# Projections finished by token block, K, Q and V in another order, and a router that reads raw x

## The reference

```python
h = modulate(rms_norm(x, norm_mix[0]), sh_m, sc_m)      # h * (1 + scale) + shift
x = x + g_m * retention(h, ...)                          # ends in (silu(g) * on) @ ret_w_out
x = x + g_f * swiglu(modulate(rms_norm(x, norm_ff[0]), sh_f, sc_f), ff_w_in, ff_w_out)
k, v = split(modulate(rms_norm(x, kv_norm), sh_kv, sc_kv) @ kv_w)
h = modulate(rms_norm(x, norm_mix[1]), sh_m1, sc_m1)
x = x + g_m1 * stick_breaking(h, k, v, sb_w_q, sb_w_out) # 16 heads of 64, strictly causal
h = modulate(rms_norm(x, norm_ff[1]), sh_f1, sc_f1)
logits = h @ router                                      # top 2 of 8 experts, softmax of the two
x = x + g_f1 * sum_e gate[:, e] * swiglu(h, moe_w_in[e], moe_w_out[e])
return rms_norm(x, final_norm)
```

## Time and profile before

| | |
|---|---|
| median of 3 runs | 1656.91 us (1653.4 to 1657.97) |
| the profiled execution | 1656.74 us, span 1655.0 us |
| TensorE busy | 1562.3 us, 94% |
| VectorE busy | 1407.4 us, 85% |
| ScalarE busy | 1074.0 us, 65% |
| GpSimd busy | 59.6 us, 4% |
| mean granted clock of TensorE | 0.976 |
| moved by DMA | 500.91 MB, mean 303 GB/s |

### The profile page before, as it was taken

How to read it: one execution, slowest core, us unless ns; L and a number is a source line. 1 busy time by engine, 2 the same in 40 slices (tenths; PEclk the granted TensorE clock), 3 DMA queues, 4 the chain that set the end, 5 groups by cost and what they waited for, 6 DMA issues and landing times.

```text
span 1655.0 us, 22753 instructions
## 1 busy us (share of the span) xinstructions
PE 1562.3 (94%) x7324; PEld 1296.9 (78%) x7324; DVE 1407.4 (85%) x1537; ACT 1074.0 (65%) x1164; POOL 59.6 (4%) x47
## 2 busy tenths in 40 slices
PE   5999997999979896999999999999999999999996
PEld 4788775888869665888888888888888888888884
DVE  6988987788887745898998998998998998999994
ACT  3454433444355535787787787787887877878783
POOL 0212200000000110000000000000000000000000
PEclk9999998999989996999999999999999999999998
DMA  9977776788847321899999999999999999999991
GB/s 333 348 249 263 253 272 219 254 309 297 317 164 268 102 77 51 325 388 347 358 376 345 359 368 355 358 372 356 349 376 348 358 379 343 362 373 338 366 380 53
DMA packets 235114, 500.91 MB, mean 303 GB/s; under 512 B 9744, under 2 KB 40640, under 8 KB 235072
## 3 DMA queue, kind: packets, MB, share of 16 engines
q1 hardware_dynamic: 233904, 500.29, 83.9%
q10 hardware_dynamic: 1168, 0.07, 0.0%
HBM read 499.28 MB, written 1.05 MB: 302 GB/s over the span
## 4 chain that ended last, share of the span: by engine, by line
PE 83%; DVE 8%; issue 3%; DMA 2%; ACT 2%; POOL 1%; DVEq 0%; SPq 0%; ACTq 0%; POOLq 0%
PE ps L492 24%; PE ps L494 24%; PE ps L493 24%; DVE w_lo L1358 2%; DVE acc L1377 2%; DMA ada<-in_ada_w 2%; PE ps L908 1%; PE ps L726 1%; PE ps L730 1%; PE ps L728 1%; DMA raw<-in_ret_w_in 1%; PE ps L525 1%; PE ps L917 1%; PE ps L941 0%; PE ps L918 0%
## 5 line engine op out<-in xcount | busy, mean ns | idle before, releaser
L1358 DVE TENSOR_TENSOR w_lo<-raw,w_hi 128x1024 fp32r<-128x1024 f32 x834 | 994.2, 1230 | 83.5 <-ACT w_hi L1006 69.4
L1006 ACT ACTIVATE w_hi<-raw 128x1024 fp32r<-128x1024 f32 x834 | 865.6, 1060 | 254.7 <-PE ps L494 216.8
L492 PE MATMUL ps<-w_hi,RA 128*128 128x512 f32 x1528 | 607.2, 397 | 12.0 <-DVE w_lo L1358 2.9
L494 PE MATMUL ps<-w_hi,RA 128*128 128x512 f32 x1528 | 598.5, 392 | 0.0
L493 PE MATMUL ps<-w_lo,RA 128*128 128x512 f32 x1528 | 597.9, 391 | 0.0
L492 PEld LDWEIGHTS ps<-w_hi,RA 128*128 128x128 f32 x1528 | 288.7, 189 | 71.5 <-issue 3.2
L494 PEld LDWEIGHTS ps<-w_hi,RA 128*128 128x128 f32 x1528 | 288.5, 189 | 61.6
L493 PEld LDWEIGHTS ps<-w_lo,RA 128*128 128x128 f32 x1528 | 288.9, 189 | 58.4 <-issue 0.5
L492 PE MATMUL ps<-w_hi,hT_hi 128*128 128x512 f32 x400 | 160.6, 401 | 7.7 <-DVE hT_lo L1428 6.9
L494 PE MATMUL ps<-w_hi,hT_lo 128*128 128x512 f32 x400 | 157.4, 393 | 0.0
L493 PE MATMUL ps<-w_lo,hT_hi 128*128 128x512 f32 x400 | 157.3, 393 | 0.0
(11 more groups left out here) (232 smaller groups left out, 1021.7 us busy)
## 6 DMA issues: line engine op xcount, KB each, us to landing
raw<-in_moe_w_in SPq DMA_DIRECT2D x224, 1024.0 KB
raw<-in_moe_w_out SPq DMA_DIRECT2D x112, 1024.0 KB
ada<-in_ada_w SPq DMA_DIRECT2D x46, 1024.0 KB, 7.3
raw<-in_ff_w_in SPq DMA_DIRECT2D x44, 512.0 KB
raw<-in_ret_w_in SPq DMA_DIRECT2D x16, 1024.0 KB
raw<-in_ff_w_out SPq DMA_DIRECT2D x11, 1024.0 KB
raw<-in_ret_w_in SPq DMA_DIRECT2D x16, 512.0 KB
raw<-in_ret_w_out SPq DMA_DIRECT2D x8, 1024.0 KB
```

The costliest lines, as they stand in the source:

```text
L492: pe.matmul(out, a_hi, b_hi, start=first, stop=False)
L494: return pe.matmul(out, a_lo, b_hi, start=False, stop=last)
L1006: act.activation(w_hi[:, cn % RING, cols], raw[:, cn % RAW, cols], ACT.Copy).then_inc(hi_done, 1)
L1358: v.tensor_tensor(w_lo[:, cn % RING, cols], raw[:, cn % RAW, cols], w_hi[:, cn % RING, cols].bitcast(f32), ALU.subtract).then_inc(lo_done, 1)
```

## The change

Projections by block: the last halves of each output projection are gone through for block 0, then for block 1, and gating, root, norm, transposes and modulation are done per block. The transposes of a block are put between matmuls of the other. The first tile after it goes by block too.

```diff
-            for m in range(8):
+            for m in range(5):
...
+            block_rows(U_OUT + 5, rT_hi, rT_lo, 10, 0, 0, False, False)
+            pe.wait_ge(gbc_ev, 1)
+            reduce_ada(11, 4)
+            pe.wait_ge(rTl_ok, PAIRS)
+            block_rows(U_OUT + 6, rT_hi, rT_lo, 12, 0, 0, False, False)
+            block_rows(U_OUT + 7, rT_hi, rT_lo, 14, 0, 0, False, True).then_inc(y_ok, 1)
+            block_rows(U_OUT + 5, rT_hi, rT_lo, 10, 1, 2, False, False)
+            reduce_ada(12, 5)
+            block_rows(U_OUT + 6, rT_hi, rT_lo, 12, 1, 2, False, False)
+            transpose_x(1, 0)
+            block_rows(U_OUT + 7, rT_hi, rT_lo, 14, 1, 2, False, True)
...
+                    block_half(c, 0, 0, 0, 1)
+                    transpose_x(1, 1)
+                    block_half(c, 1, 0, 0, 1)
+                    block_half(c, 0, 1, 1, 1)
+                    block_half(c, 1, 1, 1, 1)
```

VectorE's order there (ScalarE's follows it), with all eight steps of unit 13 behind block 1:

```diff
-            woven(26, 0, (8, 12), 12, (0, 6))
+            woven(26, 0, (8, 12), 12, (0, 8))
             mod_out(11, 4)
...
+            add_gated(0, 0, gate_m, f_tmp)
+            split_quarters(U_FF, 0, 0, 1)
+            normed(1, 0)
+            split_quarters(U_FF, 0, 1, 2)
             mod_out(12, 5)
...
+            modulate(1, 1, 0, FF0 + SH)
+            split_quarters(U_FF, 0, 2, 3)
+            add_gated(0, 1, gate_m, f_tmp)
+            split_quarters(U_FF, 0, 3, 4)
+            normed(1, 1)
+            split_quarters(U_FF, 0, 4, 6)
+            modulate(1, 1, 1, FF0 + SH)
+            ada_steps(13, 0, 8)
```

```diff
+            halves = [(kv_w, h, D) for h in range(2)]
+            halves += [(w, h, t * TW) for t in range(2) for w in (kv_w, sb_w_q[0]) for h in range(2)]
+            halves += [(kv_w, h, D + TW) for h in range(2)]
+            halves += [(sb_w_out[0], h, t * TW) for h in range(2) for t in range(2)]
+            ada_after = {0: (22, 0), 1: (22, 1), 3: (23, 0), 4: (23, 1), 6: (24, 0), 8: (24, 1), 10: (25, 0), 11: (25, 1),
+                         13: (26, 0), 14: (26, 1)}
...
+            out_block(0, 0)
+            out_block(0, 1).then_inc(y_ok, 1)
+            pe.wait_ge(gbc_ev, 3)
+            reduce_last(25)
+            reduce_last(26)
+            out_block(1, 0)
...
+            transpose_raw(0)
+            out_block(1, 1)
...
+            route(0)
+            transpose_raw(1)
             broadcast_gate(3, diag3, 2)
+            route(1)
```

The buffers of the pairs rotate over three places instead of four, the gate's diagonal moves on GpSimd from before the masks to between masks 5 and 6. The router multiplies raw x (transposed by `transpose_raw`) by router weights that carry scale and gain (`rws`), multiplies by the reciprocal root and adds the shift's part (`sh_e`) afterwards:

```diff
+                    last = pe.matmul(ps[:, 6 + b, 0:NE], h32[:, b, kc, :], rws[:, kc, :], start=kc == 0,
+                                     stop=kc == KC - 1)
...
+                ins = v.scalar_tensor_tensor(logit[:, b, :], ps[:, 6 + b, 0:NE], stat[:, 6 + b:7 + b], sh_e, ALU.mult,
+                                             ALU.add)
```

```diff
             def gathered_high(ne):
                 act.wait_ge(hgT_done, ne + 1)
-                act.activation(hg_hi.rearrange("p (n c) s -> p n (c s)", n=2), ps[:, 6:8, :], ACT.Copy)\
-                   .then_inc(hgh_ok, 1)
+                for c in range(4):
+                    ins = act.activation(hg32[:, c, :], ps[:, 6, c * P:(c + 1) * P], ACT.Identity,
+                                         bias=modc[:, FF1 + SH + c:FF1 + SH + c + 1], scale=scol[:, 4, c:c + 1])
+                ins.then_inc(hg32a_ok, 1)
+                act.wait_ge(hg32a_ok, ne + 1)
+                act.activation(hg_hi[:, 0:4, :], hg32[:, 0:4, :], ACT.Copy).then_inc(hgh_ok, 1)
+                act.wait_ge(hg32b_ok, ne + 1)
+                act.activation(hg_hi[:, 4:8, :], hg32[:, 4:8, :], ACT.Copy).then_inc(hgh_ok, 1)
...
             def gathered_low(ne):
-                dve.wait_ge(hgh_ok, ne + 1)
-                v.tensor_tensor(hg_lo.rearrange("p (n c) s -> p n (c s)", n=2), ps[:, 6:8, :],
-                                hg_hi.rearrange("p (n c) s -> p n (c s)", n=2).bitcast(f32),
-                                ALU.subtract).then_inc(hgl_ok, 1)
+                dve.wait_ge(hgT_done, ne + 1)
+                for c in range(4, KC):
+                    ins = v.tensor_scalar(hg32[:, c, :], ps[:, 7, (c - 4) * P:(c - 3) * P], scol[:, 4, c:c + 1],
+                                          modc[:, FF1 + SH + c:FF1 + SH + c + 1], ALU.mult, ALU.add)
+                ins.then_inc(hg32b_ok, 1)
+                for i in range(2):
+                    dve.wait_ge(hgh_ok, 2 * ne + i + 1)
+                    v.tensor_tensor(hg_lo[:, 4 * i:4 * i + 4, :], hg32[:, 4 * i:4 * i + 4, :],
+                                    hg_hi[:, 4 * i:4 * i + 4, :].bitcast(f32), ALU.subtract).then_inc(hgl_ok, 1)
```

More of the change, by code:

```diff
@@ L41 @@
 U_KV = U_FF + 3 * FT
[L42 to L44 removed]
+U_SBO = U_KV + 12
 U_MOE = U_SBO + 4
@@ L603, in pair_of_heads @@
                     pe.wait_ge(mod_ok, 2 * i + 1)
-                tile(0, m, (0, 1), None if later else 0)
+                if later:
+                    tile(0, m, (0, 1))
+                else:
+                    tile_by_blocks(0, (0, 1), 0)
                 if later:
@@ new lines, in route @@
+            def route(b):
+                pe.wait_ge(xra_ok, b + 1)
+                pe.wait_ge(xrb_ok, b + 1)
+                for kc in range(KC):
+                    last = pe.matmul(ps[:, 6 + b, 0:NE], h32[:, b, kc, :], rws[:, kc, :], start=kc == 0,
+                                     stop=kc == KC - 1)
+                last.then_inc(rt_done, 1)
+            transpose_raw(0)
+            out_block(1, 1)
+            pe.wait_ge(rws_ok, 1)
+            pe.wait_ge(xra_ok, 1)
+            pe.matmul(ps[:, 6, 2 * NE:3 * NE], ones[:, :], shw[:, :], start=True, stop=True)
@@ L1343, in _ @@
                 y_high(ne)
-            root_mean_square(4)
+            root_table()
+            for b in range(NB):
+                root_mean_square(4, b)
         @block.vector
@@ L1724, in _ @@
+            steps.link(ins)
             for b in range(NB):
```

681 lines of the change are left out of this document (367 added, 314 removed).

## The result

The changed kernel takes 1626.38 us (median of 4 runs, 1625.24 to 1628.77), the kernel before 1656.28 beside it (1653.4 to 1657.97): ratio 0.9825, 95% interval 0.9809 to 0.9841. Forecast were 1637 us and a range of 1628 to 1650. The profiled execution took 1626.12 us, span 1624.4.

The account below looks back on a forecast made before the run. TensorE was taken as the bound, with serial chains behind projections as its waits and VectorE having little room. 0.6 - 2.6 - 6.5 - 10.5 + 0 - 0.6 = -19.6 from 1656.9 gave 1637 us, range 1628 to 1650.

Parts of the forecast that it names:

- Part 1: First tile by blocks: four scalings of 128 columns on ScalarE, not two of 256, before the first matmul: +0.6 us.
- Part 2: Retention projection into the dense mixer: -4.2 us by VectorE's queue, less 1.6 charged for clock: -2.6 us.
- The clock's 1.6: Charge of 1.6 us for low clock behind the two waits of some 4 us before the first SwiGLU product.
- Parts 3 and 4: Dense mixer into K, Q, V, then attention: shorter waits let the output projection end sooner, together -6.5 us.
- Part 5: Router and gather: 24 us instead of 34.5 from the last projection matmul to the first expert matmul: -10.5 us.
- Part 6: Experts: added scalings and lows on VectorE (+1.8 us per expert) and ScalarE (+2.0) fit the room: 0 us.
- Part 7: End of the kernel: the first block's root and scaling lie beside the second's square: -0.6 us.
- (b): Better covered than counted: attention's waits vanish (-6 us) and the broadcast runs at full clock: 1628 us, chance 0.11.
- (a): Short waits keep the clock down and VectorE's queue sets the pace: +8 us, 1645 us, chance 0.19.
- (c): Block 1's chain starts as late as both blocks' did, and routing waits anyway: within 5 us of 1657, chance 0.05.
- (d): Scaling in the experts overruns its room, so TensorE waits in each of 7 experts: +27 us, 1664 us, chance 0.07.

Follow-up runs that it names:

- before_again: The kernel before, unchanged, profiled a second time: median 1654.38 us, span 1651.3 us.
- after_scale_twice: The changed kernel with the eight scalings of each gathered block made twice, the first time into a spare place: 1631.83 us.
- after_warm: The changed kernel with idle transposes of the unit matrix put into six of TensorE's waits, some 70% of each: 1620.55 us.
- before_warm: The kernel before with idle transposes of the unit matrix in seven of TensorE's waits: 1645.21 us.
- after_rows_whole: The changed kernel with the last three halves of the retention's output projection gone through for both blocks together again: 1634.04 us.
- after_out_first: The changed kernel with all matmuls of attention's output projection before block 0's transposes: 1632.68 us.
- after_tile_first: The changed kernel with TensorE taking the very first tile through both blocks together, once both are scaled: 1632.06 us.
- before_diag_late: The kernel before with GpSimd making the first gate's diagonal only after the last silu of the gates: 1650.35 us.

## Why the prediction was wrong

The waits went where each part said, and the sum was 10.6 us short. Two steps of it failed: the execution that it starts from, worth 3.6 us, and the prices of its terms, worth 7.0. Had the sum started from before_again (1653.0 us), the same terms would have given 1633.4 and a range down to 1624.4, with 1626.4 inside; from that kernel's median of 1654.4 they would have given 1634.8 and 1625.8. By its own steps, with the misses of the table:

- **Part 1 and what stands before it, 3.4 us: the step that failed most.** "+0.6" held at its place (43.92 to 44.61). But I made the sum against one execution, which lay 0.2 us from a median of three runs, as if it were typical. Two w_lo of 2.32 and 2.92 us in it were an accident, as before_again shows: there the w_lo of 240.89 comes at 236.89, so that the first line of the table reads +1.2 (0.6 above its forecast) and not -2.8, and every later stage is as long as in the table within 0.2 us. Of the 4.0 us, 2.4 are there at the wait of 205.15, and 1.6 are the slow starts behind it, which also come without a long w_lo (after_scale_twice). I used them as a price of the clock and never looked at what VectorE did before. Against before_again's span (1651.3) the change gains 26.9 us.
- **Part 2, 2.2 us, the largest of the mis-sized terms.** VectorE's chain from the first quarter to the first SwiGLU transposes took 40.4 us, not 42.6. The scalings of 128 columns had no row, and I took 0.44 and 0.40 where 0.37 and 0.34 were paid; with their lows and waits they took VectorE 2.7 us for each block, where the sum has 3.4 and 2.9 (1.0 us). The first four quarters with eight product steps took 10.1 us, not 10.7: quarters last 1.23 us but the next instruction starts after 1.14, and the sum adds whole durations there, and 1.2 us for each of the eight quarters behind. The clock's 1.6 came as 1.5. The two waits measured 3.80 and 2.97 where I said some 4 each.
- **Parts 3 and 4, 1.5 us.** V starts 14.6 us behind the mixer's last half, as forecast within 0.4. The waits in attention sum to 6.2 us, where 6.7 were counted and 8 charged with handovers: the charge on top was wrong, and the half us that I took off for it was too little.
- **Part 5, 1.3 us.** 22.7 us, forecast 24 of 23.3 to 25.2. Gate and add (2.8), the transposes (1.8) and the routing (1.9) came as forecast, and the broadcast held TensorE for 2.45 us (607.84 to 610.29) against 1.9 to 3.8. The wait of the top-2 chain was 2.15 and not 2.7, and from the counting to the first expert matmul 11.7 us passed, not 12.2.
- **Part 6, 1.0.** TensorE's 123 us per expert held. The gain is clock at the first expert's start: 9 slow starts for 14.
- **Part 7, 1.4.** The last matmuls behind the wait of 2.89 us ran 1.1 us sooner by the clock (seven slow starts for thirteen), which the sum didn't have and nothing here explains. What is left for the roots' order is 0.9, not 0.6; no run tests it alone.

The misses of parts 2 to 5 share a sign, because at each open price I took the dearer end and then added handovers; those of parts 1, 6 and 7 share it by the accident and the clock. That 1637 was too high by 10.6 rather than 7 is therefore bad luck. Of the rivals, (b) named the right side with the wrong places: attention's waits didn't vanish, and the broadcast did not run wholly at the full clock. (a) fell: after_warm shows that 5.3 us of clock could be had back in the changed kernel, but the kernel before pays more of it (8.5 us in before_warm). (c) and (d) fell with the result itself; after_rows_whole and after_out_first show that the overlap by blocks is real, and after_scale_twice that the experts had room.

## To carry to other kernels

Cut the chain behind a projection by token block and put one block's chain beside the other's matmuls: here two such places cost 8 and 7 us when the overlap was taken back. At the very first tile the same cut cost 0.7 us. Before making a sum against one execution, take a second execution, look for instructions of a common shape that took twice their group's mean, and ask what GpSimd did there. Where a wait can't be removed, fill most of it with harmless matmuls: 5 us here for six lines, 8.5 in the kernel before.

## What was not expected of the hardware

- Two executions of the same program differed by 4.0 us at 237 us of the span: 2.4 by the order in which VectorE and GpSimd started (GpSimd's product 0.03 us ahead of one VectorE instruction or 0.18 behind another), 1.6 by slow starts behind it.
- A wait of 2.18 or 2.19 us before the same matmuls cost clock in some executions and none in others: slow starts behind it in 3 of 10 traces (before, after_scale_twice, after_tile_first), none in the other 7, the changed kernel, after_warm and after_rows_whole among them. So too behind the 1.22 us at the dense mixer's first tile (ten slow starts in before_again, none in before_diag_late). It is worth 1.6 to 2.1 us a time, as much as several of the edits here gain. What decides it stays open; no run here tells.
- Small matmuls at a wait's side can be worth their time: moving 2.6 us of broadcast out of the path made the path no shorter.
